# A two-block layer on one core: the C table placed by VectorE, and a new order at the start of the first attention

## The reference, cut to what matters

```python
h = rms_norm(x, norm_g) * (1 + scale) + shift          # scale, shift, gate from c @ w_ada
q, kcr, vcr, ksl, vsl, kwn, vwn, z_a, g_br, u, z_s = split(h @ w_in)
kc = rms_norm(compress(kcr, ...)); vc = compress(vcr, ...)
attn = g0 * o_cmp + g1 * o_slc + g2 * o_win            # each softmax(q k) v, 8 heads of 64, gated by a sigmoid
attn = attn * silu(z_a)
# s5_mixer: 32 groups of 16 channels, 64 complex states each
s_t = lam_bar * s_{t-1} + b_bar u_t ;  y_t = real(c_mat s_t) + d * u_t
y = gelu(y); y = y * sigmoid(y @ glu_w + glu_b)
x = x + gate * (concat(attn, y * silu(z_s)) @ w_out)
```

## Time and profile before

| | us |
|---|---|
| median of 3 runs | 1001.34 (1001.03 to 1002.61) |
| the profiled execution's own time | 1001.67 |
| its span, first to last instruction | 999.9 |
| busy: PE, DVE, ACT, POOL | 945.0, 576.9, 459.9, 66.6 |
| mean granted TensorE clock | 0.984 of 2.4 GHz |

### The profile page before, as it was taken

One profiled execution on the slowest core, in us unless ns is written; L12 is line 12 of the kernel. 1 busy time (PEld: TensorE's weight loads), 2 busy tenths in 40 slices (PEclk: granted clock), 3 DMA queues, 4 the chain that ended last, 5 costly groups with the idle time before them and its releaser, 6 DMA issues.

```text
span 999.9 us, 14238 instructions
## 1 busy us (share of the span) xinstructions
PE 945.0 (95%) x5545; PEld 740.4 (74%) x5545; DVE 576.9 (58%) x1173; ACT 459.9 (46%) x973; POOL 66.6 (7%) x82
## 2 busy tenths in 40 slices
PE   3998999999899999999999998999999999999996
PEld 1688879774556778887788886788888678886784
DVE  5897597464898455254964436436153975334732
ACT  4637322353577324433853437534243763435730
POOL 0001002000440000000010000000000000000000
PEclk9999999999999999999899999999999899998999
DMA  9854354408400023352123323122343123323102
GB/s 359 291 128 147 63 151 144 146 22 246 156 1 2 22 85 122 85 147 85 58 86 106 86 104 127 60 85 85 85 127 105 59 86 85 99 91 106 65 1 84
DMA packets 94644, 104.66 MB, mean 105 GB/s; under 512 B 15809, under 2 KB 64961, under 8 KB 94562
## 3 DMA queue, kind: packets, MB, share of 16 engines
q1 hardware_dynamic: 90466, 87.67, 28.3%
q0 software_dynamic: 3824, 15.73, 4.9%
q10 hardware_dynamic: 288, 0.36, 0.1%
HBM read 98.37 MB, written 4.19 MB: 103 GB/s over the span
## 4 chain that ended last, share of the span: by engine, by line
PE 84%; ACT 5%; DVE 4%; DMA 3%; issue 2%; SPq 0%; DVEq 0%; POOL 0%; POOLq 0%; ACTq 0%; PEldq 0%
PE bank L1013 78%; PE bank L1315 2%; PE bank L1333 2%; ACT ring L923 2%; DMA ring<-in_w_in 1%; DMA ring<-in_w_ada 1%; DMA ring<-in_cmp_w_v 1%; ACT soft L930 1%; PE bank L1471 1%; PE bank L1389 1%; ACT w_hi L873 0%; ACT arena L704 0%; ACT hT_hi L855 0%; PE bank L1379 0%; ACT soft L807 0%
## 5 line engine op out<-in xcount | busy, mean ns | idle before, releaser
L2054 DVE TENSOR_TENSOR w_lo<-ring,w_hi 128x1024 fp32r<-128x1024 f32 x80 | 97.7, 1225 | 114.7 <-ACT w_hi L873 111.6
L1013 PE MATMUL bank<-w_hi,hT_hi 128*128 128x512 f32 x320 | 125.3, 392 | 1.3 <-issue 1.0
L1013 PE MATMUL bank<-hT_hi,w_hi 128*128 128x512 f32 x320 | 125.7, 393 | 0.0
L1013 PE MATMUL bank<-hT_lo,w_hi 128*128 128x512 f32 x320 | 124.6, 389 | 0.0
L1013 PE MATMUL bank<-w_lo,hT_hi 128*128 128x512 f32 x320 | 124.6, 389 | 0.0
L1013 PE MATMUL bank<-hT_hi,w_lo 128*128 128x512 f32 x320 | 124.5, 389 | 0.0
L1013 PE MATMUL bank<-w_hi,hT_lo 128*128 128x512 f32 x320 | 124.5, 389 | 0.0
L873 ACT ACTIVATE w_hi<-ring 128x1024 fp32r<-128x1024 f32 x80 | 84.4, 1058 | 11.7 <-PE bank L1013 11.4
L1013 PEld LDWEIGHTS bank<-w_hi,hT_hi 128*128 128x128 f32 x320 | 60.1, 188 | 14.7 <-issue 2.6
L1013 PEld LDWEIGHTS bank<-hT_hi,w_hi 128*128 128x128 f32 x320 | 60.1, 188 | 13.1 <-issue 0.7
L1013 PEld LDWEIGHTS bank<-w_lo,hT_hi 128*128 128x128 f32 x320 | 60.1, 188 | 12.6
(11 more groups left out here) (313 smaller groups left out, 1817.2 us busy)
## 6 DMA issues: line engine op xcount, KB each, us to landing
ring<-in_w_in SPq DMA_DIRECT2D x66, 512.0 KB, 4.3
ring<-in_w_ada SPq DMA_DIRECT2D x4, 2048.0 KB, 14.3
ring<-in_w_in SPq DMA_DIRECT2D x4, 2048.0 KB, 8.5
bias_ring<-in_na_bias POOLq DMA_DIRECT2D x8, 1024.0 KB, 5.4
ring<-in_w_out SPq DMA_DIRECT2D x16, 512.0 KB, 3.5
ring<-in_w_out SPq DMA_DIRECT2D x2, 2048.0 KB, 9.7
bias_ring<-in_t_bias POOLq DMA_DIRECT2D x8, 448.0 KB, 3.6
x_t<-in_x SPq DMA_DIRECT2D x4, 512.0 KB, 5.9
```

Source lines behind the costliest of these rows:

```text
L1013: return pe.matmul(out, lhsT, rhs, start=first, stop=last)
L2054: dve.tensor_tensor(w_lo[:, u % 4], raw_w[:, u % 4], w_hi[:, u % 4].bitcast(fp32), SUB).then_inc(S["w_split"], 1)
```

## The change

1. DVE writes the C table into `cl` itself. The real part goes straight into the even groups' places of `cl` on all 128 partitions, whose lower half (64 to 127) holds the odd groups for the moment; ACT moves only those (one copy of 64 x 2304, to partitions 0 to 63). The imaginary part is formed by two subtractions of 64 partitions each, the second of which waits for ACT's copy (`cl_moved` 5). `move_cl` goes. PE waits for `cl_moved` 5 and `cl_ready` 2.
2. The V products wait for `kk_evac` 6 ahead of the real and 8 ahead of the imaginary half.
3. `score_1(1)` stands right behind the GLU and ahead of the transposes of the compressed weights, and these go into banks 0 and 1. `turn_1(0)`, which uses the same banks, waits for `cp_evac`.
4. On ACT `exps_1(0)` stands ahead of the last GLU tanh, `exps_1(1)` right behind it, and in the loop the evacuations of j-2 stand ahead of `exps_1(j)`.
5. On DVE the start of the attention is written out: takes 0, `ssm_out(0)`, takes 1, `ssm_out(1)`, `scale_1(0)`, `ssm_out(2)`, and `ssm_out(3)` at j = 2.

```diff
-            def move_cl(part):
-                act.wait_ge(S["cl_ready"], part + 1)
-                cl5 = cl.rearrange("p (g u m) -> p g u m", g=GP, u=2)
-                for two in range(2):
-                    act.activation(cl5[part * SN:(part + 1) * SN, :, two, :],
-                                   cut(cl_tmp[two * SN:(two + 1) * SN, :], g=GP, m=(LC + 1) * SC), ACT.Copy).then_inc(S["cl_moved"], 1)
...
-            move_cl(0)
+            act.wait_ge(S["cl_ready"], 1)
+            cl4 = cl.rearrange("p (g u m) -> p g u m", g=GP, u=2)
+            act.activation(cl4[0:SN, :, 1, :], cl4[SN:P, :, 0, :], ACT.Copy).then_inc(S["cl_moved"], 1)
...
-            move_cl(1)
...
             for f in range(4):
+                if f == 3:
+                    exps_1(0)
                 act.wait_ge(S["glu_done"], f + 1)
...
-            exps_1(0)
+            exps_1(1)
             for n in range(2):
                 act.wait_ge(S["cp_T"], n + 1)
-                act.activation(cpT[:, n, :], bank[2 + n][:, :], ACT.Copy).then_inc(S["cp_evac"], 1)
+                act.activation(cpT[:, n, :], bank[n][:, :], ACT.Copy).then_inc(S["cp_evac"], 1)
...
             for j in range(n + 2):
-                if 1 <= j < n:
-                    exps_1(j)
                 if j >= 2:
...
                         act.activation(probT1_of(k)[:, 0:width], bank[k % 2][:, 0:width], ACT.Copy).then_inc(S["t1_evac"], 1)
+                    if j < n:
+                        exps_1(j)
...
-            pe.wait_ge(S["cl_moved"], 8)
+            pe.wait_ge(S["cl_moved"], 5)
+            pe.wait_ge(S["cl_ready"], 2)
...
-            pe.wait_ge(S["kk_evac"], 8)
             pe.wait_ge(S["u_back"], 16 * LC)
             wr, wi = (cut(v, g=GP, m=P) for v in (w_re, w_im))
             for part, w in enumerate((wr, wi)):
+                pe.wait_ge(S["kk_evac"], 6 + 2 * part)
...
-                    if j == 1:
-                        pe.wait_ge(S["cp_evac"], 2)
...
             pe.sem_inc(S["w_free"], 1)
+            pe.wait_ge(S["glu_tanh"], 3)
+            score_1(1)
...
             pe.wait_ge(S["cp_ready"], 1)
-            pe.wait_ge(S["glu_tanh"], 3)
+            pe.wait_ge(S["cs_taken"], 2)
...
-                    ins = pe.transpose(bank[2 + n][:, a * P:(a + 1) * P], soft[:, o:o + P], ident)
+                    ins = pe.transpose(bank[n][:, a * P:(a + 1) * P], soft[:, o:o + P], ident)
...
                     if j:
                         pe.wait_ge(S["t1_evac"], k - 1)
+                    else:
+                        pe.wait_ge(S["cp_evac"], k + 1)
...
-                if 1 <= j < n:
+                if 2 <= j < n:
                     score_1(j)
...
-            dve.tensor_tensor(ca, ca, cb, SUB).then_inc(S["cl_ready"], 1)
+            cl5 = cl.rearrange("p (g u j c) -> p g u j c", g=GP, u=2, j=LC + 1, c=SC)
+            dve.tensor_tensor(cl5[:, :, 0], ca, cb, SUB).then_inc(S["cl_ready"], 1)
             dve.wait_ge(S["cl_ready"], 1)
             tt(cb, powers(pw_re, LC + 1), over(c_im, LC + 1), MUL)
             part_lo(11)
-            dve.wait_ge(S["cl_moved"], 6)
             tt(ca, powers(pw_nim, LC + 1), over(c_re, LC + 1), MUL)
-            dve.tensor_tensor(ca, ca, cb, SUB).then_inc(S["cl_ready"], 1)
+            tt(cl5[SN:P, :, 1], ca[SN:P], cb[SN:P], SUB)
+            dve.wait_ge(S["cl_moved"], 5)
+            dve.tensor_tensor(cl5[SN:P, :, 0], ca[0:SN], cb[0:SN], SUB).then_inc(S["cl_ready"], 1)
...
-            for j in range(n + 4):
+            def take_1(j):
...
+            take_1(0)
+            ssm_out(0)
+            take_1(1)
+            ssm_out(1)
+            scale_1(0)
+            ssm_out(2)
+            for j in range(2, n + 4):
                 if j < n:
...
+                    take_1(j)
+                if j <= n:
                     scale_1(j - 1)
-                if 1 <= j < 5:
-                    ssm_out(j - 1)
+                if j == 2:
+                    ssm_out(3)
```

More of the change, by code:

```diff
@@ L791, in _ @@
                         .then_inc(S["y_tanh"], 1)
[L793 to L799, removed]
             def exps_1(j):
@@ L808, in exps_1 @@
                         .then_inc(S["e1_done"], 1)
-            exps_1(0)
+            for f in range(4):
+                if f == 3:
+                    exps_1(0)
+                act.wait_ge(S["glu_done"], f + 1)
+                act.activation(cut(uT, f=4, t=T)[:, f, :], bank[GLU_BANKS[f]][:, :], ACT.Tanh, scale=0.5,
+                               bias=glu_hb[:, f:f + 1]).then_inc(S["glu_tanh"], 1)
+                if f == 1:
+                    act.wait_ge(S["cs_ready"], 1)
+                    act.activation(soft[:, 0:1024], soft[:, 0:1024], ACT.Exp, scale=SCALE).then_inc(S["cs_exp"], 1)
+            exps_1(1)
             for n in range(2):
                 act.wait_ge(S["cp_T"], n + 1)
-                act.activation(cpT[:, n, :], bank[2 + n][:, :], ACT.Copy).then_inc(S["cp_evac"], 1)
+                act.activation(cpT[:, n, :], bank[n][:, :], ACT.Copy).then_inc(S["cp_evac"], 1)
             def move_gate(c, part):
@@ L2033, in _ @@
             dve.wait_ge(S["causal_in"], 16)
-            for j in range(n + 4):
-                if j < n:
[L2036 to L2043, removed]
+            def take_1(j):
+                width = (PAIRS1[j][0] + 1) * P
+                for k in (2 * j, 2 * j + 1):
+                    dve.wait_ge(S["s1_done"], k + 1)
+                    if k >= 8:
+                        dve.wait_ge(S["t1_done"], k - 7)
+                    dve.tensor_tensor_reduce(prob1_of(k)[:, 0:width], bank[S_BANKS[k % 4]][:, 0:width], causal[:, T - width:T],
+                                             -SCALE, 3.0e38, ADD, MIN, negm[:, k % 8:k % 8 + 1]).then_inc(S["s1_taken"], 1)
+            take_1(0)
[5 more added lines that the diff above has]
+            for j in range(2, n + 4):
+                if j < n:
+                    take_1(j)
+                if j <= n:
                     scale_1(j - 1)
-                if 1 <= j < 5:
-                    ssm_out(j - 1)
+                if j == 2:
+                    ssm_out(3)
                 if j >= 4 and (j - 3) % PER_I == 0:
```

## The result

The changed kernel takes **987.65 us** (median of 4 runs, 986.78 to 988.82), the one before took 1001.18 beside it (1000.68 to 1002.61): a ratio of 0.9863, 95% interval 0.9846 to 0.9880, 13.5 us less. I had forecast 990.5, so the sign and most of the size were right; 2.8 us of gain were not foreseen, and the result lies at the very edge of my range (987.5 to 995.0). The profiled execution took 988.49 us (span 986.7), against 1001.67 (span 999.9): 13.2 us.

A forecast was written before the change was run, and what follows sets the result against it. PE bounds the kernel (945.0 us busy, 84% of the chain), so only its holes or low clock pay. Part A 5.8 + Part B 5.0 = 10.8 us, from 1001.34 to 990.5 us; range 987.5 to 995.0.

The forecast's parts named there:

- the order inside ACT's loop: Attention steps: evacuating j-2 before exponentials of j taken as 0; bounds 0.3 us a step lost, 1.5 us gained.
- Part A: C table and V gate, 94 to 111 us: hole closes, V starts at 105.1 instead of 110.98; 5.8 us carried.
- Rival 1: Behind the C table's transposes the clock falls all the same; price 1.9 us, 992.4 us, chance 0.13.
- Rivals 3 and 5: At attention's start Part B closes no hole, 995.5, chance 0.05; at the C table Part A does nothing, 996.3, chance 0.04.
- Rival 4: Steps 8 to 31: ACT's turned order makes PE wait for exponentials, 0.63 a step, 15 us; 1005.6 us, chance 0.03.
- Part B: Attention's start: new order closes the hole ahead of turn 1; 3.3 us by scores 8, 5.0 us in all.
- The new hole: Ahead of PE's gate sum: scores 1 no longer cover ACT's copy of the gate parts; 0.6 us lost.
- POOL: POOL's earlier split slows DVE in 512-wide steps: PE loses 0.6 at turn 2, 0.3 at turn 4, 0.8 at turn 6.
- Scores 8 to 12: 384-wide attention steps, freed of POOL's split: 14.4 us becomes 12.7, a gain of 1.7.
- Rival 2: 512-wide attention steps: POOL slows DVE, PE loses 1.5 more and the late 1.7 gain goes; 993.7 us, chance 0.13.
- The clock's term: Low clock behind the two holes goes: 1.9 us in Part A, 1.4 us in Part B.

The follow-up runs named there:

- e2: The changed kernel with the C table and V gate edits undone, leaving the new order at the attention's start alone; 995.14 us, ratio 0.9945.
- e3: The changed kernel with ACT's loop back in the old order, exponentials of pair j ahead of evacuations of j-2; 990.63 us, ratio 0.9897.
- e9: The kernel before with ACT's order turned round for the 256 and 128 wide pairs alone (j from 16 on); 999.08 us, ratio 0.9972.
- e5: The changed kernel with the V products waiting for all eight kernel evacuations again; 989.38 us, ratio 0.9888.
- e1: The kernel before with only the C table placed by DVE and the V products' gate split; 993.35 us, ratio 0.9936.
- e8: The changed kernel with PE's first gate sum put behind the scores of pair 2 instead of ahead; 987.74 us, ratio 0.9869.
- e11: The changed kernel with POOL's whole split held back until DVE has taken the attention's last scores; 1000.92 us in one run.
- e4: The kernel before with ACT's loop alone turned round, evacuations of j-2 ahead of exponentials of j from j = 2; 998.45 us, ratio 0.9979.
- e6: The changed kernel with ssm_out(3), which releases POOL's split, put back two steps to step 4 of DVE's loop; 988.61 us, ratio 0.9892.

## Why the prediction was right, and where it was wrong

**The step that failed: the order inside ACT's loop.** The prediction says: "I take 0, with ... 1.5 us of gain (small waits of the narrow steps) below." It measured 2.3 us (scores 12 to the projection, 42.78 to 40.46), 2.05 in e2 without part A, 2.0 when taken out of the change and 1.65 for j = 16 on in the kernel before. It is the largest single part of the missing gain and past the bound that I had set. (The other bound, 0.3 us over 24 steps, is 7.2 us and would end at 997.7, outside my range of 987.5 to 995.0, which claimed to take in the far ends.) My working was a loop of averages: 1.25 us a step through four engines against ACT's 1.36, hence ACT-bound, hence order without effect. But ACT wasn't saturated: from scores 12 to the projection of the kernel before it is busy for 33.0 of 42.8 us. In a step of the kernel before it waits for DVE's take, then does exponentials, then the evacuation that PE needs. The turned rows lie finished meanwhile. Timeline of ACT of e3, whose old order shows it:

```profile
314.93 0.40 ACT L792 ACTIVATE arena<-arena,small 128x128 f32<-128x128 f32 x1 [0.86 <-DVE small L2043]
...
315.72 0.42 ACT L838 ACTIVATE soft<-bank 128x128 f32<-128x128 f32 x2
```

and PE's turn behind it, at 316.12, waits 0.42 us for that evacuation. In an in-order queue the time that counts is the wait of what stands in front, not the sum of the work. I had read PE's waits as one sum over 400 us, where the 2.6 of one hole hides the small ones of the narrow steps; the same view of 300 to 345 us, shown with e9, has them.

**Part A: right.** V at 104.83, forecast 105.1. The transposes close up, the two 64-partition subtractions take 2.56 and 2.55, the 0.68 goes by the V gate alone (e5). The kernel products took 7.16 for 7.0. SP's Toeplitz DMAs are issued from 102.12, 5.4 earlier.

**Rival 1, the clock falls all the same: wrong.** 3.69 us of nothing but transposes ran at 1.00 and left the clock at 1.00. By the Trainium skill ("TensorE: Matmul & The Clock Gate", section "Part 4: PE-mode transpose") transposes don't count as a busy PE; these fp32 transposes, behind a full stretch of products, show no sign of it. None of the eight kernels with this hole closed has a fall between 94 and 111 us.

**Rivals 3 and 5** fell with e2 and e1: each part does its own work. **Rival 4** had its place right and its sign wrong: the exponentials that now wait for a turn make nobody wait.

**Part B up to scores 8: 2.19 for 3.3.** Three pieces. The new hole was foreseen as 0.6 and is 0.72, but taking it away gives 1.16 (e8), as 0.4 of waits on DVE's scale goes with it. POOL was put at 0.6 + 0.3 + 0.8 = 1.7 and cost 1.64 (e11). What is left is the gross gain: 3.3 + 0.6 + 1.7 = 5.6 forecast, 2.19 + 1.16 + 1.64 = 5.0 measured, if the pieces add, which no run with both edits at once shows.

**Scores 8 to 12: 2.18 for 1.7.** I had the old steps in part as bound by other things than POOL; they were nearly all POOL (14.39 against 11.79 in e11). **Rival 2**, that POOL gives B back, is wrong as a sum and right as a mechanism: 2.06 us are still paid, where B as a whole gains 4.37 to scores 12. The Trainium skill ("SBUF — State Buffer", section "Who interferes with whom") says that when DVE and GpSimd want their shared ports, the second comer is blocked for the whole of the other's instruction. The pairs of 1.81 to 2.82 us instead of 1.00 agree: their excess of 0.8 to 1.8 is of the order of the POOL instruction beside them (0.61 to 2.44). That POOL is the cause e11 shows; that it is the ports no run here separates.

**The clock's term** was taken as certain: 1.9 in A and 1.4 in B. One fall costs 1.71, as both did in the profiled execution before, so their sum of 3.3 was near the 3.4 measured; but e2 shows that the first needn't come. A gain in clock is thus a gain in some executions.

**Sum.** 6.15 - 0.03 + 2.19 + 2.18 + 2.32 + 0.39 = 13.2 against 10.8: A 0.3 more (6.1 for 5.8), B to scores 12 0.6 less, ACT's order 2.3 more, behind the projection 0.4 more. That last term isn't the change's: e1 and e2 have 665.07 and 666.77 there, against 667.44 in the kernel before, so it moves by over 2 us where the code is the same, and the late falls of the clock differ with it. Why the late falls differ from one kernel to the next stays open.

## What to carry to other kernels

Where a queue mixes work that waits for different engines, put first the item that the bottleneck waits for, and judge the order by what each item waits for, not by sums per step; it paid 1.7 to 2.3 us here, over sixteen to twenty steps in which ACT had time to spare. One wait removed can uncover the next: the order alone turned a hole of 2.61 us on ACT into one of 1.77 on DVE (e4). A reorder also changes which steps a GpSimd task lies beside; price both places, as the task costs PE something in each (e6: 1.65 gained, 2.17 lost). Where two executions differ by a fall of the clock, take it out before crediting an edit: in e4 most of a gain of 2.4 was that. Look for the work that used to cover a copy when you move it (the gate sum: a hole of 0.72, worth 1.16).

## What the runs showed of the hardware

- The same idle time of 3.32 us ahead of the same transposes was followed by a fall to 1.2 GHz in the kernel before, e4 and e9, and by none in e2. The idle time of 2.6 us ahead of turn 1 was followed by one in the kernel before, e1 and e9, all three that have it; the 1.77 of e4 in that place by none. Where it fell the moment differed: in e4 the clock was already down when PE took up work again, in e9 it went down 1 us later. Windows of e4 and of e9:

```profile
99.00:100.00 1.00, 0.02 (x1) 0.03 (x1) 0.00 (x0) 0.98 (x3) 1.00 (x1) 0.77 1.10 382
100.00:101.00 1.00, 1.00 (x5) 1.00 (x6) 0.00 (x0) 1.00 (x3) 1.00 (x1) 0.50 1.10 348
```

```profile
99.00:100.00 1.00, 0.32 (x3) 0.32 (x4) 0.00 (x0) 0.97 (x3) 1.00 (x1) 1.00 1.10 367
100.00:101.00 1.00, 1.00 (x10) 0.86 (x8) 0.00 (x0) 1.00 (x4) 1.00 (x1) 0.80 1.11 350
```

- Nearly every fall lost 1.7 us or twice that (8.5 in e11, behind its long wait, and 1.9 to 3.3 in the closing microseconds). Single times of one kernel lie up to 8 us apart (before: 998.91 at a mean clock of 0.987, 1006.8 at 0.976), while the stretches from V to the output projection agree to 0.3 where the code and the falls are the same. The stretch up to V does not: it ends between 104.83 and 105.89 in the seven kernels with the same code up to there, and the five from 105.36 on all have a fall at 31 us. So a term of 1 us is better read in a stretch than in a median.
- A subtraction of 64 partitions takes as long as one of 128: 2.56 us for 2304 elements in a row either way (the earlier trace rows and part A above).
